# Joined column parts in three more jobs of the first MLP product, and one norm sum without spreading

## The chip, the cores and the metric

The kernel runs on one core of a Trainium2 chip. The metric is the device time of one execution in microseconds, the median of several. The engines are called as the profile calls them: PE (TensorE), DVE (VectorE), ACT (ScalarE), POOL (GpSimd), and SP, which here only issues DMAs.

## The reference

One encoder layer over 1536 tokens (a prompt sequence of 1024 and a sample sequence of 512), width 1024, all in float32:

```python
h = rms_norm(x, g_mix) * (1.0 + scale1) + shift1
z = h @ w_in                                  # 1024 x 1536
y_f = fourier_mixer(u_f, w_fourier)
y_r = bidirectional_rglru(conv(u_r), ...) * jax.nn.gelu(u_g)
mix = jnp.concatenate([y_f, y_r], axis=-1) @ w_out
x = x + gate1 * mix

h = rms_norm(x, g_mlp) * (1.0 + scale2) + shift2
ff = jnp.square(jax.nn.relu(h @ w_ff1)) @ w_ff2   # 1024 -> 4096 -> 1024
return x + gate2 * ff
```

and a last RMSNorm. shift, scale and gate come from a small product with the conditioning vector. The change lies in the second `rms_norm` and in `h @ w_ff1`.

## The kernel before

Activations lie transposed, 128 channels on the partitions and the tokens along the free dimension. The tokens are cut into three chunks of 512, taken in the order 0, 2, 1. Each engine has its own program, written out by hand in the order in which it runs; semaphores tie them together, and an engine that waits holds back everything behind it in its program.

**Products in two halves.** A float32 product is made of numbers split in a high part (`_hi`, rounded to fp32r) and a low part (`_lo`, the remainder): low weights by high data, high weights by low data, high by high (`three`, `three_of`, line 843 to 845). ACT makes the high part by a copy, DVE or POOL the low one by a subtraction (`split_w1_hi` on ACT, `w1_split_lo` on POOL, `token_lo` on DVE).

**The second norm.** While the output projection runs over its three chunks, ACT squares the new x, DVE adds the squares into `n_acc`, PE sums over the partitions (`norm_sum`), ACT takes the root (`root`), DVE the reciprocal (`rstd`), and DVE scales x (`norm_apply`). For the first chunk (n = NN) the sum is one product with the matrix of ones as weights and the 512 columns of `n_acc` as data, so that each partition has the sum of each column, and the reciprocal is one of 128x512. For the second and third chunk the sum is four products with 128 columns of `n_acc` as weights, the root and the reciprocal are of four columns, and PE spreads them to all partitions by four more products with the unit matrix (`norm_spread`, line 879).

**The first MLP product** uses a scheme of seven products for a 2x2 block product (Strassen and Winograd's): the tokens are halved into 768 columns each, the weights into blocks. There are 17 jobs: job 0 and job 5 are one pair of blocks in two halves, with 512 and with 256 columns; the other jobs have 768 columns, in two parts of 512 and 256 (a PSUM bank holds 512 columns of float32). In a job PE makes the seven products in the order P1, P5, P6, P2, P7, P3, P4 (i = 0 to 6), `ff1_product(q, i)`. P1, P6, P7 and P4 are added up in one PSUM buffer, and ACT copies the state of it after each (`ff1_out`, line 1636; semaphore `ff1_copy`). From these copies and the buffers of P5, P2 and P3 DVE makes the seven hidden blocks (`hid_out`, semaphore `hid_step`), in the steps U2, C11, B11, C22, B22, C12, B12, T1, T3, T2, T4; SP stores each to DRAM (`store_hid`, line 698). The weights of a product are in a ring of four places (`w1_hi`, `w1_lo`, `w1_s`); POOL makes the sums of weight blocks that P5, P6, P7 and P3 need (`w1_add`), but in job 5 DVE makes those of P7 and P3. SP loads the weights of the next job (`load_w1`, line 685), in its one queue between the stores.

**Joined parts.** In jobs 6 to 15 the part of 256 columns is done by `grouped` (line 854 and 857): four matmuls of 512 columns, high weights by high and low data side by side, and four of 256 columns, low weights by high data, which are added to the high columns. The result lies in two halves of 256 columns that DVE must add: `add_low(q, i)` (line 2294), and for P4 `relu_square(q)` on DVE, which in the other jobs is part of ACT's relu and square. The semaphore `ff1_added` counts these nine. In a joined job P6, P7 and P4 on PE wait for the addition of the product ahead of them in the same buffer, and P2 of the next job for that of P4; the store of the block `S_B21` waits for `relu_square`:

```python
if step: ...
else:
    sp.wait_ge(ff1_sq, q + 1)
    if QH <= q < NJ - 1:
        sp.wait_ge(ff1_added, added(q, SQ_P4))
```

For job 5 SP's order is: store of S_B21 of job 4, loads of job 6 (A11, A21, A22), store of S_T4 of job 4, load of A12.

Of the kernel before, what the change touches and what calls it, by code (L numbers as in the profile page):

```python
# [30 lines left out]
F32 = mybir.dt.float32  # L31
# [41 lines left out]
ADDED = (P1, P6, P5, P2, P7, A_P5, P3, P4, SQ_P4)  # L73
QH = REST + 2
U2, C11, B11, C22, B22, C12, B12, T1, T3, T2, T4 = range(1, 12)
# [73 lines left out]
def build_encoder(nc, vec_d, xT_d, w_mod_d, w_mod1_d, w_in_d, w_gate_d, w_four_d, w_out_d, w_ff1_d, w_ff2_d,  # L149
# [163 lines left out]
    n_acc = place("n_acc", [P, CH], F32, s2 + 2048)  # L313
    n_rstd = place("n_rstd", [P, CH], F32, A0 + HALF)
    n_sq = tmp[:2]
# [187 lines left out]
    def added(q, i):  # L503

        return len(ADDED) * (q - QH) + ADDED.index(i) + 1

# [31 lines left out]
    def spread_count(n):  # L538

        return n + 1 if n < NN else n  # L540

# [53 lines left out]
    def _(sp):  # L595
# [91 lines left out]
        def store_hid(q, j, step):  # L687

            pair, c0, c1 = JOBS[q]
            if step:  # L690
                sp.wait_ge(hid_step, NHID * q + step)
                if q == 0 and step in (B11, B22):
                    sp.wait_ge(first_relu, 2 if step == B11 else 6)
            else:
                sp.wait_ge(ff1_sq, q + 1)
                if QH <= q < NJ - 1:
                    sp.wait_ge(ff1_added, added(q, SQ_P4))
            sp.dma_start(hid_d[j, :, pair, c0:c1], hid_tile(j, q)[:, c0:c1]).then_inc(st_hid[j], 16)
# [135 lines left out]
    def _(pe):  # L834
# [26 lines left out]
        def norm_sum(n):  # L861

            pe.wait_ge(sq_added, adds_v(n + 1))
            if NN < n < 2 * NN:
                pe.wait_ge(xn_done, xn_count(n))
            if n == NN:
                pe.matmul(norm_bank(n)[:], ones[:], n_acc[:], start=True, stop=True).then_inc(norm_mm, 1)
                return
            total = squares(n)[:, 0, :] if shared(n) else n_acc[:]
            for b in range(4):  # L870
                m = pe.matmul(norm_bank(n)[:, b * P:(b + 1) * P], total[:, b * P:(b + 1) * P], ones[:],
                              start=True, stop=True)
            m.then_inc(norm_mm, 1)
# [238 lines left out]
        for i in range(1, NCH):  # L1112
            for d in range(KD):
                n = (i - 1) * KD + d

                pe.wait_ge(out_evac, n % 6 + 1 if n < 6 else KD + n - 5)
                if i == 2 and d == 0:
                    pe.wait_ge(mixr_lo, FT * 2)
                out_half(ORDER[i], d, 0, n % 6, True, False)
                if i == 2 and d == 0:  # L1120
                    norm_sum(NN + 1)
                out_half(ORDER[i], d, 1, n % 6, False, True).then_inc(out_mm, 1)
                if i == 1 and d == 0:
                    pe.wait_ge(out_evac, KD)
                    norm_sum(NN)
                elif i == 2 and d == 0:
                    norm_spread(NN + 1)

        def ff1_product(q, i):
# [10 lines left out]
            if i == P1:  # L1140
                after(pe, hid_step, NHID * (q - 1) + C11)
            elif i == P5:
                after(pe, hid_step, NHID * (q - 1) + C22)
            elif i == P2:
                after(pe, ff1_copy, 4 * q)
                if q > QH:
                    pe.wait_ge(ff1_added, added(q - 1, P4))
            elif i == P3:
                after(pe, hid_step, NHID * (q - 1) + C12)
            else:  # L1150
                pe.wait_ge(ff1_copy, 4 * q + {P6: 1, P7: 2, P4: 3}[i])
                if QH <= q < NJ - 1:
                    pe.wait_ge(ff1_added, added(q, {P6: P1, P7: P6, P4: P7}[i]))
# [4 lines left out]
            for part in parts:  # L1158
# [3 lines left out]
                begin = i in (P1, P5, P2, P3)  # L1162
                if part == 1 and QH <= q < NJ - 1:
                    m = grouped(ps[:, buf + CH:buf + 2 * CH],
                                [(w1_hi[o % 4][:, kk * P:(kk + 1) * P], w1_lo[o % 4][:, kk * P:(kk + 1) * P])
                                 for kk in range(FT)], lambda kk: pair[:, :, kk], begin, True)
                    continue
# [116 lines left out]
    def _(act):  # L1284
# [21 lines left out]
        def root(n):  # L1306
            act.wait_ge(norm_mm, n + 1)
            after(act, rc_done, n)
            if n == NN:
                act.activation(n_rstd[:], norm_bank(n)[:], ACT.Sqrt, bias=eps[:], scale=1.0 / D).then_inc(sd_done, 1)  # L1310
                return
            act.activation(sd[:], norm_bank(n)[:, 0:CH:P], ACT.Sqrt, bias=eps[:], scale=1.0 / D
                           ).then_inc(sd_done, 1)
# [308 lines left out]
        def ff1_out(q, i, j, step):  # L1622
# [4 lines left out]
            if q > 1 or i != P1:  # L1627
                after(act, hid_step, NHID * (q - 1) + step)
                after(act, st_hid[j], 16 * q)
            if i == P4 and QH <= q < NJ - 1:  # L1630
                act.activation(hid[j][:, CH:HTOK], ps[:, buf + CH:buf + HTOK], ACT.Copy)
# [200 lines left out]
        for d in range(2):  # L1832
            scale_small(d)
        act.wait_ge(norm_bc, 2 * NN + 2)
        act.activation(fin_s[:], bank[3][:, 0:QC], ACT.Copy).then_inc(small_r, 1)
# [6 lines left out]
    def _(dve):  # L1842
# [20 lines left out]
        def rstd(n):  # L1863

            dve.wait_ge(sd_done, n + 1)
            if n == NN:
                dve.reciprocal(n_rstd[:], n_rstd[:]).then_inc(rc_done, 1)
                return
# [336 lines left out]
        def norm_apply(n, tiles=range(KD)):  # L2205

            c = chunk_of(n)
            s = SEQ_OF[c]
            if n == NN:
                dve.wait_ge(rc_done, n + 1)  # L2210
            else:
                dve.wait_ge(norm_bc, spread_count(n))
            scale = n_rstd if n == NN else norm_bank(n)
            for k in tiles:
# [87 lines left out]
        def hid_out(q, step):  # L2302
# [8 lines left out]
            slot, at = [hid_tile(j, q) for j in range(7)], NHID * q  # L2311
            if QH <= q < NJ - 1 and step in (U2, C11, C22, C12, T4):
                dve.wait_ge(ff1_added, added(q, {U2: P5, C11: P2, C22: A_P5, C12: P3, T4: SQ_P4}[step]))
# [135 lines left out]
        def fin_rstd(h):  # L2449

            dve.wait_ge(sd_done, 2 * NN + h + 1)
            after(dve, norm_bc, (2 * NN - 1 + h) * h)
            dve.reciprocal(rc_half[:], sd_half[:]).then_inc(rstd_done, 1)
# [8 lines left out]
        def final_first(tiles):  # L2462

            dve.wait_ge(norm_bc, 2 * NN)
            final(tiles, 0, HTOK, ps[:, 6 * CH:6 * CH + HTOK])
# [6 lines left out]
        def final_small():  # L2472

            dve.wait_ge(norm_bc, 2 * NN + 1)
            r = bank[7][:, 0:QC].unsqueeze(1).to_broadcast([P, 2, QC])
# [31 lines left out]
        for q in range(1, NJ):  # L2507
            low = {U2: (P1, P6, P5), C11: (P2,), C22: (P7, A_P5), C12: (P3,)} if QH <= q < NJ - 1 else {}
            for step in (U2, C11, B11, C22, B22, C12, B12, T1, T3, T2):
# [4 lines left out]
                hid_out(q, step)  # L2514
            if QH <= q < NJ - 1:
                add_low(q, P4)
                relu_square(q)
            if q == REST:
                w1_add(q + 1, P7)
                w1_add(q + 1, P3)  # L2520
            hid_out(q, T4)

# [240 lines left out]
```

## Time and profile before

| | us |
|---|---|
| median of 3 runs (1399.94 to 1400.83) | 1400.32 |
| profiled execution | 1399.79 |
| its span, first to last instruction | 1397.5 |
| PE busy | 1376.4 (98%) |
| DVE busy | 848.4 (61%) |
| ACT busy | 586.6 (42%) |
| POOL busy | 477.7 (34%) |

The granted clock of PE is 0.999 over the span. The columns of a timeline are start in us from the span's start, duration in us, engine, line, operation, output<-input, shape and count; in brackets stands the idle time ahead of it and what ended it. Durations of matmuls overlap: it is the distance of their starts that counts.

### The profile page before, as it was taken

What the parts mean: (1) busy time and instruction counts of PE and PEld (TensorE: products, weight loads), DVE (VectorE), ACT (ScalarE), POOL (GpSimd) and SP (SyncE); (2) the same over time, 40 slices, a digit from 0 to 9 for tenths busy, and PEclk for the clock granted to TensorE, in tenths of its full rate; (3) what the DMA queues carried; (4) which work ended last, traced back from release to release, by engine and by line L of the source; (5) the groups of instructions that cost most, each with busy time, mean ns of one, the idle gap of its engine ahead of it and who ended that gap; (6) DMA issues with size and microseconds to landing.
All of it is one profiled execution on the core that took longest, in us unless ns stands there. A gap on an engine that the chain in (4) does not pass through costs nothing.

```text
span 1397.5 us, 17631 instructions
## 1 busy us (share of the span) xinstructions
PE 1376.4 (98%) x7050; PEld 1155.7 (83%) x7050; DVE 848.4 (61%) x871; ACT 586.6 (42%) x713; POOL 477.7 (34%) x269
## 2 busy tenths in 40 slices
PE   5999999999999999999999999999999999999998
PEld 4877778898888888888888888888888888888887
DVE  5967688795538974566545564453746434354584
ACT  5667888665325632232222222342322223423252
POOL 0002111145003775574554545531432222332131
PEclk9999999999999999999999999999999999999999
DMA  9444411106311343343433344479997444445552
GB/s 369 170 159 158 152 68 38 46 26 209 128 61 31 118 165 121 132 148 140 155 127 116 126 146 151 163 286 388 387 382 277 151 151 158 171 174 196 199 187 91
DMA packets 75698, 231.25 MB, mean 165 GB/s; under 512 B 5729, under 2 KB 9953, under 8 KB 66786
## 3 DMA queue, kind: packets, MB, share of 16 engines
q1 hardware_dynamic: 75074, 229.60, 44.9%
q8 instruction: 57, 0.93, 0.3%
q10 hardware_dynamic: 544, 0.52, 0.1%
q14 instruction: 23, 0.19, 0.0%
HBM read 165.09 MB, written 65.01 MB: 165 GB/s over the span
## 4 chain that ended last, share of the span: by engine, by line
PE 96%; DVE 2%; DMA 1%; issue 1%; SPq 1%; ACT 0%; POOL 0%; DVEq 0%; ACTq 0%
PE bank L844 17%; PE bank L843 17%; PE bank L845 17%; PE bank L854 10%; PE bank L837 9%; PE bank L838 9%; PE bank L839 9%; PE bank L857 5%; PE bank L889 1%; DMA win_raw<-in_w_in 1%; PE bank L901 0%; DVE two_r L2245 0%; SPq L604 0%; PE bank L910 0%; DVE n_t L2217 0%
## 5 line engine op out<-in xcount | busy, mean ns | idle before, releaser
L2387 DVE TENSOR_TENSOR hin_two<-hin,hin_two 128x3072 fp32r<-128x3072 f32 x28 | 131.4, 4694 | 185.7 <-ACT hin_two L1700 185.7
L2664 POOL TENSOR_TENSOR w_lo<-w_raw,w_hi 128x2048 fp32r<-128x2048 f32 x28 | 134.9, 4817 | 318.8 <-ACT w_hi L1688 317.2
L843 PE MATMUL bank<-hin_two,w_lo 128*128 128x512 f32 (+1 forms) x576 | 211.2, 367 | 0.0
L844 PE MATMUL bank<-hin_two,w_hi 128*128 128x512 f32 (+1 forms) x576 | 210.9, 366 | 0.0
L845 PE MATMUL bank<-hin_two,w_hi 128*128 128x512 f32 (+1 forms) x576 | 210.9, 366 | 0.0
L1688 ACT ACTIVATE w_hi<-w_raw 128x2048 fp32r<-128x2048 f32 x28 | 53.6, 1913 | 247.6 <-PE bank L857 149.5
L2656 POOL TENSOR_TENSOR w_lo<-w_raw,w_hi 128x512 fp32r<-128x512 f32 x43 | 63.3, 1473 | 180.1 <-ACT w_hi L1620 180.0
L845 PEld LDWEIGHTS bank<-hin_two,w_hi 128*128 128x128 f32 x576 | 108.6, 189 | 17.7
L843 PEld LDWEIGHTS bank<-hin_two,w_lo 128*128 128x128 f32 x576 | 108.7, 189 | 17.4 <-issue 0.2
L844 PEld LDWEIGHTS bank<-hin_two,w_hi 128*128 128x128 f32 x576 | 108.6, 189 | 17.4 <-issue 0.2
L2294 DVE TENSOR_TENSOR hid<-bank,hid 128x256 f32<-128x256 f32 x80 | 33.9, 424 | 124.2 <-ACT hid L1636 105.2
L2656 POOL TENSOR_TENSOR w_lo<-w_s,w_hi 128x512 fp32r<-128x512 f32 x68 | 105.0, 1561 | 7.2 <-ACT w_hi L1620 4.8
L2590 POOL TENSOR_TENSOR win_lo<-win_raw,win_hi 128x1024 fp32r<-128x1024 f32 x10 | 26.6, 2662 | 212.8 <-ACT win_hi L1325 212.8
L1636 ACT ACTIVATE hid<-bank 128x768 f32<-128x768 f32 (+2 forms) x58 | 44.4, 765 | 127.9 <-PE bank L845 82.0
L1700 ACT ACTIVATE hin_two<-hin 128x3072 fp32r<-128x3072 f32 x28 | 77.2, 2759 | 44.3 <-DMA hin<-hid_all 44.3
L844 PE MATMUL bank<-t_two,w_hi 128*128 128x512 f32 (+1 forms) x240 | 88.6, 369 | 0.0
L845 PE MATMUL bank<-t_two,w_hi 128*128 128x512 f32 (+1 forms) x240 | 88.6, 369 | 0.0
L843 PE MATMUL bank<-t_two,w_lo 128*128 128x512 f32 (+1 forms) x240 | 88.5, 369 | 0.0
L1620 ACT ACTIVATE w_hi<-w_s 128x512 fp32r<-128x512 f32 x68 | 43.0, 632 | 107.8 <-POOL w_s L2646 48.8
L854 PE MATMUL bank<-hin_two,w_hi 128*128 128x512 f32 x320 | 86.9, 393 | 0.0
L2332 DVE SCALAR_TENSOR_TENSOR hid<-hid 128x768 f32<-128x768 f32 (+1 forms) x48 | 66.1, 1377 | 1.7
L843 PE MATMUL bank<-two_f,w_lo 128*128 128x512 f32 (+1 forms) x176 | 63.6, 362 | 0.8 <-DVE hid L2321 0.4
(326 smaller groups left out, 3373.4 us busy)
## 6 DMA issues: line engine op xcount, KB each, us to landing
hin<-hid_all SPq DMA_DIRECT2D x28, 1536.0 KB, 6.7
hid_all<-hid SPq DMA_DIRECT2D x105, 384.0 KB, 2.4
w_raw<-in_w_ff SPq DMA_DIRECT2D x36, 1024.0 KB, 9.0
mod_raw<-in_w_mod SPq DMA_DIRECT2D x16, 1024.0 KB, 6.3
w_raw<-in_w_ff SPq DMA_DIRECT2D x60, 256.0 KB, 3.5
x<-in_xT SPq DMA_DIRECT2D x5, 2048.0 KB, 14.5
w_sums<-w_raw SPq DMA_DIRECT2D x8, 1024.0 KB, 15.5
w_raw<-w_sums SPq DMA_DIRECT2D x8, 1024.0 KB, 9.7
```

The source lines that it names most:

```text
L837: pe.matmul(out, w_lo, v_hi, start=first, stop=False)
L838: pe.matmul(out, w_hi, v_lo, start=False, stop=False)
L839: return pe.matmul(out, w_hi, v_hi, start=False, stop=last)
L843: pe.matmul(out, w_lo, v_hi, start=first, stop=False, skip_group_check=True)
L844: pe.matmul(out, w_hi, v_lo, start=False, stop=False, skip_group_check=True)
L845: return pe.matmul(out, w_hi, v_hi, start=False, stop=last, skip_group_check=True)
L854: pe.matmul(out.rearrange("p (h n) -> p h n", h=2), w_hi, v(t), start=first and t == 0, stop=False, skip_group_check=True)
L857: m = pe.matmul(out[:, HI * QC:(HI + 1) * QC], w_lo, v(t)[:, HI], start=False, stop=last and t == len(weights) - 1, skip_group_check=True)
L1700: act.activation(hin_part(n % 3, HI), hin[n % 3][:].rearrange("p t n -> p (t n)"), ACT.Copy).then_inc(hin_hi_done, 1)
L2387: dve.tensor_tensor(hin_part(n % 3, LO), hin[n % 3][:].rearrange("p t n -> p (t n)"), hin_part(n % 3, HI), ALU.subtract).then_inc(hin_lo_d ...
L2656: pool.tensor_tensor(w1_lo[o % 4][:], src[:], w1_hi[o % 4][:], ALU.subtract).then_inc(w1_lo_done, 1)
L2664: pool.tensor_tensor(w2_lo[n % 2][:].rearrange("p t n -> p (t n)"), w2_raw[m % RAWS][:].rearrange("p t n -> p (t n)"), w2_hi[n % 2][:].rea ...
```

## The change

Two changes. The list of joined jobs, before all from 6 to 15, becomes `JOINED`, jobs 2, 3, 4 and 6 to 15; every place that asked for `QH <= q < NJ - 1` asks for `q in JOINED`. In job 4 DVE's two weight sums for job 5 now stand ahead of its addition of P4 and its relu-square. And the second chunk of the second norm (n = NN + 1) is summed like the first, by one product with ones, with a root and a reciprocal of 128x512 and no `norm_spread`; the counts on `norm_bc` fall by one.

```diff
-QH = REST + 2
+JOINED = tuple(q for q in range(2, NJ - 1) if q != REST + 1)
...
-    n_rstd = place("n_rstd", [P, CH], F32, A0 + HALF)
+    n_rstd = [place(f"n_rstd{i}", [P, CH], F32, o) for i, o in enumerate((A0 + HALF, A0 + 2 * HALF + 11 * 2048))]
...
-        return len(ADDED) * (q - QH) + ADDED.index(i) + 1
+        return len(ADDED) * JOINED.index(q) + ADDED.index(i) + 1
...
-        return n + 1 if n < NN else n
+        return min(n + 1, NN) if n < NN + 2 else n - 1
...
-                if QH <= q < NJ - 1:
+                if q in JOINED:
                     sp.wait_ge(ff1_added, added(q, SQ_P4))
...
-            if n == NN:
+            if n in (NN, NN + 1):
                 pe.matmul(norm_bank(n)[:], ones[:], n_acc[:], start=True, stop=True).then_inc(norm_mm, 1)
                 return
...
                 if i == 1 and d == 0:
                     pe.wait_ge(out_evac, KD)
                     norm_sum(NN)
-                elif i == 2 and d == 0:
-                    norm_spread(NN + 1)
...
             elif i == P2:
                 after(pe, ff1_copy, 4 * q)
-                if q > QH:
+                if q - 1 in JOINED:
                     pe.wait_ge(ff1_added, added(q - 1, P4))
...
-                if QH <= q < NJ - 1:
+                if q in JOINED:
                     pe.wait_ge(ff1_added, added(q, {P6: P1, P7: P6, P4: P7}[i]))
...
-                if part == 1 and QH <= q < NJ - 1:
+                if part == 1 and q in JOINED:
                     m = grouped(ps[:, buf + CH:buf + 2 * CH],
...
-            if n == NN:
-                act.activation(n_rstd[:], norm_bank(n)[:], ACT.Sqrt, bias=eps[:], scale=1.0 / D).then_inc(sd_done, 1)
+            if n in (NN, NN + 1):
+                act.activation(n_rstd[n - NN][:], norm_bank(n)[:], ACT.Sqrt, bias=eps[:], scale=1.0 / D).then_inc(sd_done, 1)
...
-            if i == P4 and QH <= q < NJ - 1:
+            if i == P4 and q in JOINED:
                 act.activation(hid[j][:, CH:HTOK], ps[:, buf + CH:buf + HTOK], ACT.Copy)
...
-            if n == NN:
-                dve.reciprocal(n_rstd[:], n_rstd[:]).then_inc(rc_done, 1)
+            if n in (NN, NN + 1):
+                dve.reciprocal(n_rstd[n - NN][:], n_rstd[n - NN][:]).then_inc(rc_done, 1)
...
-            scale = n_rstd if n == NN else norm_bank(n)
+            scale = n_rstd[n - NN] if n < NN + 2 else norm_bank(n)
...
-            low = {U2: (P1, P6, P5), C11: (P2,), C22: (P7, A_P5), C12: (P3,)} if QH <= q < NJ - 1 else {}
+            low = {U2: (P1, P6, P5), C11: (P2,), C22: (P7, A_P5), C12: (P3,)} if q in JOINED else {}
...
-            if QH <= q < NJ - 1:
-                add_low(q, P4)
-                relu_square(q)
             if q == REST:
                 w1_add(q + 1, P7)
                 w1_add(q + 1, P3)
+            if q in JOINED:
+                add_low(q, P4)
+                relu_square(q)
             hid_out(q, T4)
```

## Rows read from the trace of the kernel before

**Rows 1.** Page, busy us, share of the span, instructions of each engine.

```profile
PE 1376.4 (98%) x7050; PEld 1155.7 (83%) x7050; DVE 848.4 (61%) x871; ACT 586.6 (42%) x713; POOL 477.7 (34%) x269
```

**Rows 2.** PE's waits, whole run: who for whom, us in total, times, longest us.

```profile
PE bank L843 <- DVE hid L2321: 0.4, 1, 0.4
...
PE bank L843 <- POOL w_lo L2656: 0.4, 1, 0.4
```

**Rows 3.** PE's timeline, job 2: start us, us, what; parts apart.

```profile
524.04 0.28 PE L843 MATMUL bank<-two_f,w_lo 128*128 128x256 f32 x1
...
532.38 0.28 PE L843 MATMUL bank<-t4b_two,w_lo 128*128 128x256 f32 x1
...
532.50 0.28 PE L844 MATMUL bank<-t4b_two,w_hi 128*128 128x256 f32 x1
```

**Rows 4.** PE's timeline, job 6: starts of two joined groups.

```profile
613.99 0.39 PE L854 MATMUL bank<-t_two,w_hi 128*128 128x512 f32 x1
...
622.26 0.62 PE L854 MATMUL bank<-two_f,w_hi 128*128 128x512 f32 x2
```

**Rows 5.** PE's timeline at the norm's sums and its spreading.

```profile
369.50 1.02 PE L867 MATMUL bank<-n_acc,ones 128*128 128x512 f32 x2
...
370.59 0.40 PE L838 MATMUL bank<-lo_r,wo_hi 128*128 128x512 f32 x1
...
411.21 1.05 PE L871 MATMUL bank<-ones,n_acc 128*128 128x128 f32 x8
...
414.83 1.05 PE L879 MATMUL bank<-ident,rc 128*128 128x128 f32 x8
...
415.95 0.39 PE L838 MATMUL bank<-lo_r,wo_hi 128*128 128x512 f32 x1
```

**Rows 6.** DVE's timeline: first reciprocal, x of the third chunk, idle in brackets.

```profile
371.28 3.35 DVE L1867 RECIPROCAL n_rstd<-n_rstd 128x512 f32<-128x512 f32 x1 [0.76 <-ACT n_rstd L1310]
...
415.03 0.75 DVE L2257 SCALAR_TENSOR_TENSOR x<-bank,mod,x 128x512 f32<-128x512 f32 x1 [2.20 <-PE bank L839]
...
454.04 0.75 DVE L2257 SCALAR_TENSOR_TENSOR x<-bank,mod,x 128x512 f32<-128x512 f32 x1 [1.89 <-PE bank L839]
```

**Rows 7.** Timelines of DVE and PE where job 2 begins.

```profile
512.61 0.96 DVE L2354 TENSOR_TENSOR hid<-hid,hid 128x768 f32<-128x768 f32 x1
...
512.98 0.39 PE L843 MATMUL bank<-t_two,w_lo 128*128 128x512 f32 x1
```

**Rows 8.** Page: group of the additions of 256 columns.

```profile
L2294 DVE TENSOR_TENSOR hid<-bank,hid 128x256 f32<-128x256 f32 x80 | 33.9, 424 | 124.2 <-ACT hid L1636 105.2
```

**Rows 9.** PE's timeline: starts of (6,P1) and (6,P5).

```profile
602.88 0.40 PE L843 MATMUL bank<-two_f,w_lo 128*128 128x512 f32 x1
...
607.02 1.19 PE L854 MATMUL bank<-t_two,w_hi 128*128 128x512 f32 x4
```

**Rows 10.** DVE's timeline, from job 4 to job 5.

```profile
595.71 0.69 DVE L2366 TENSOR_TENSOR w_s<-w_raw,w_s 128x512 f32<-128x512 f32 x1
...
596.31 0.95 DVE L2354 TENSOR_TENSOR hid<-hid,hid 128x768 f32<-128x768 f32 x1
...
598.68 1.26 DVE L2332 SCALAR_TENSOR_TENSOR hid<-hid 128x256 f32<-128x256 f32 x1
```

**Rows 11.** POOL's timeline: low halves of (5,P7) and (6,P1).

```profile
596.42 1.99 POOL L2656 TENSOR_TENSOR w_lo<-w_s,w_hi 128x512 fp32r<-128x512 f32 x1 [1.36 <-ACT w_hi L1620]
...
601.18 1.48 POOL L2656 TENSOR_TENSOR w_lo<-w_raw,w_hi 128x512 fp32r<-128x512 f32 x1
```

**Rows 12.** SP: loads of job 6; landing of its first, and of job 5's three.

```profile
595.64 0.82 SPq L685 DMA_DIRECT2D w_raw<-in_w_ff  x2
...
DMA to landing us min/median/max: 4.4/4.4/4.4
...
DMA to landing us min/median/max: 2.6/3.3/3.6
```

**Rows 13.** ACT's timeline: high half for (6,P1).

```profile
600.48 0.62 ACT L1620 ACTIVATE w_hi<-w_raw 128x512 fp32r<-128x512 f32 x1
```

More of the change, by code:

```diff
@@ L1833, in _ @@
             scale_small(d)
-        act.wait_ge(norm_bc, 2 * NN + 2)
+        act.wait_ge(norm_bc, 2 * NN + 1)
         act.activation(fin_s[:], bank[3][:, 0:QC], ACT.Copy).then_inc(small_r, 1)
@@ L2208, in norm_apply @@
             s = SEQ_OF[c]
-            if n == NN:
+            if n in (NN, NN + 1):
                 dve.wait_ge(rc_done, n + 1)
@@ L2311, in hid_out @@
             slot, at = [hid_tile(j, q) for j in range(7)], NHID * q
-            if QH <= q < NJ - 1 and step in (U2, C11, C22, C12, T4):
+            if q in JOINED and step in (U2, C11, C22, C12, T4):
                 dve.wait_ge(ff1_added, added(q, {U2: P5, C11: P2, C22: A_P5, C12: P3, T4: SQ_P4}[step]))
@@ L2451, in fin_rstd @@
             dve.wait_ge(sd_done, 2 * NN + h + 1)
-            after(dve, norm_bc, (2 * NN - 1 + h) * h)
+            after(dve, norm_bc, (2 * NN - 2 + h) * h)
             dve.reciprocal(rc_half[:], sd_half[:]).then_inc(rstd_done, 1)
@@ L2462, in final_first @@
         def final_first(tiles):
-            dve.wait_ge(norm_bc, 2 * NN)
+            dve.wait_ge(norm_bc, 2 * NN - 1)
             final(tiles, 0, HTOK, ps[:, 6 * CH:6 * CH + HTOK])
@@ L2472, in final_small @@
         def final_small():
-            dve.wait_ge(norm_bc, 2 * NN + 1)
+            dve.wait_ge(norm_bc, 2 * NN)
             r = bank[7][:, 0:QC].unsqueeze(1).to_broadcast([P, 2, QC])
```

## The prediction

> **What bounds the kernel now.** I read the page's busy shares first: TensorE (PE) is busy 98% of the 1397.5 us span, DVE 61% [rows 1]. So nothing that DVE, ACT or POOL do counts by its length, only where PE has to wait for it. Then I read PE's waits over the whole run. In the part that the change touches there are just two, of 0.4 us each: the first product of the second job waits for DVE (474 us), and a product of the sixth job waits for POOL's low half of its weights (598.5) [rows 2]. Then PE's timeline, product by product, in a job with separate parts [rows 3] and in one with joined parts [rows 4]; then DVE, POOL and SP around the places where the change puts a new wait. So each edit is priced twice: what PE issues less, and whether PE now reaches a semaphore before its giver does.
>
> I call the jobs by their number q (third to fifth are q = 2, 3, 4; q = 5 is the short one of 256 columns; q = 6 to 15 are joined already), and a product by job and name, (2,P6). Times on the clock are those of the trace of before.
>
> **Part 1, joined products on PE.** In each of the 7 products of jobs 2, 3 and 4, twelve matmuls of 256 columns become four of 512 and four of 256: the same 3072 columns, in 8 instructions and not 12. As neighbouring products run their parts in opposite order, two products make a period. Separate: from 524.04 to 532.38, 8.34 us, in which one of 256 columns takes 0.12 (532.38 to 532.50) and so one of 512 takes (8.34 - 24 x 0.12) / 24 = 0.228 [rows 3]. Joined: from 613.99 to 622.26, 8.27 us [rows 4]. So a product gains 0.035 us and 21 of them 0.7 us. I take off 0.05, because a first joined group stands between products of the other kind: **-0.65 us**. Bounds: the joining brings nothing (0), or four matmuls fewer by the price that they have over their columns, 2 x 0.120 - 0.228 = 0.012 us each, 0.05 a product: -1.05.
>
> A rule speaks against this part. The Trainium skill, "TensorE: Matmul & The Clock Gate", section "Back-to-back issue gap", gives an isolated matmul N/2.4 + 2.5 ns. By it four instructions less would save only 10 ns a product, an estimate of 0.2 us for 21, and the change would come out 0.45 us later than my sum. The rows of this kernel, 8.34 against 8.27, say 35 ns, and I go by them.
>
> **Part 2, the norm.** The spreading of the second chunk stands on PE at 414.83; to the second matmul behind it, at 415.95, pass 1.12 us, of which the first takes 0.23, so it costs 0.89. The sum at 411.21 is four products of the same shape, and I give it the same 0.89. The first chunk is already done by one product with ones as weights: 369.50 to 370.59, 1.09 - 0.23 = 0.86 [rows 5]. The change makes the sum 0.86 for 0.89 and drops the spreading: **-0.92 us**. PE's waits [rows 2] hold neither, so it is all length.
> The price is on DVE: a reciprocal of 512 columns, 3.35 us as in the first chunk, for one of 4 columns. There it began 1.78 us after the product (371.28 against 369.50, the root on ACT between them); so here it runs from 413.0 to 416.4, and what stood at 415.03 (the new x of the third chunk, then eight scalings) starts 1.4 us later [rows 6]. Those who read it are the ACT shifts and the token sums, and PE wants none of them before the first MLP product, 40 us on. DVE stands idle 1.89 us before 454.04, waiting for PE [rows 6], so it has caught up there even with PE 0.92 us ahead. I cost it at nothing; if that cover were gone, the whole 1.2 to 1.4 us would reach the second job's first product, where PE waits for DVE already. From 454 to 475 DVE works without a gap, started by PE, so that old wait moves ahead with PE and stays 0.4 us long.
>
> **Part 3, the new wait in job 2.** In a joined job DVE has to add the halves of P1 before PE may write P6 into the same buffer (the wait on ff1_added, value P1). DVE reaches job 2 late: it still has the token sums of job 1 to make, works without a gap up to the last step of job 1, T4 at 512.61, 0.96 us, and ends it at 513.57. The addition takes 0.42 us [rows 8], with the hand-over 513.6 to 514.1. PE begins (2,P6) at 512.98 [rows 7], and would by the gain of part 1 be there 0.07 us earlier. So PE waits 514.1 - 512.9: **+1.15 us**. Both sides move ahead by the same 0.92 of part 2, so it doesn't matter here. Bounds: 0.7 (DVE's chain is 0.4 us shorter because locks fall otherwise) and 1.6. Jobs 3 and 4 are cut like 7 and 8 of before, in which PE waits for nothing [rows 2], and I give them no cost.
> The edit also puts nine DVE operations into each job (eight of 0.42 us and one relu-square): 3.8 us of DVE time in seven products of 4.2. DVE has the room; only the order matters.
>
> **Part 4, jobs 4 to 6.** Job 5 has a third of a job's columns and lasts some 10 us, so what DVE, POOL and SP prepare for it and for job 6 has no slack. Three things come in. (a) PE's (5,P2) now waits for the addition of (4,P4), which DVE makes after the two weight sums: the second at 595.71, 0.69 long, so the addition ends at 596.8. Counted back from (6,P1) at 602.88 [rows 9], three products of 12 x 0.12 = 1.44 us put (5,P7) at 598.5; ahead of it are the old wait for POOL, some 0.5, and (5,P2) itself, which so began at 596.5. It now waits 0.3 us, and the old wait behind it falls. (b) relu-square of job 4 then follows on DVE, with both inputs in SBUF. At 596.42 POOL begins the low half of (5,P7); DVE's T4 of 0.95 us at 596.31 was ahead of it [rows 10] and made it last 1.99 us [rows 11]. Without T4 there I take 1.3, 0.7 less. Now POOL comes first and DVE waits: relu-square ends at 597.7 + 0.4 = 598.1. That is what the trace does to such pairs: the 256-column relu-square at 598.68 took 1.26 us beside POOL [rows 10], where an addition of that size out of PSUM takes 0.42 [rows 8]. The Trainium skill says so, "SBUF — State Buffer", section "SBUF: two separate sides": an exclusive lock for the whole instruction, which a DVE operation with two SBUF inputs and one of POOL take from each other. By that rule, the trace agrees.
> (c) SP stores job 4's square (hid, B21) first, and the weight loads of job 6 stand behind it in its queue. The store now waits for relu-square, 598.1, not for ACT's square. The load of A11 was issued at 595.64 and landed 4.4 us later, at 600.04 [rows 12]; now the store is issued first, 0.4 us as two loads took 0.82, and the load at 598.5, and lands after some 3.3 us, as the median of three such loads did at 568.7 [rows 12], at 601.8. ACT's split took 0.62 us and started at 600.48 [rows 13]; now it ends at 602.4. POOL's low half, 1.48 us [rows 11], ends at 603.9. PE began (6,P1) at 602.88 [rows 9]: now 603.9. From there POOL makes two sums and the low half of P5 without a gap, from 601.18 + 1.48 = 602.66 [rows 11] to the start of (6,P5) at 607.02 [rows 9], 4.36 us: now 603.9 + 4.36 = 608.3. **+1.25 us** at (6,P5), which takes in (a), the freed 0.5 us and what job 4's last product had gained. Bounds: the load lands in 2.6 us and POOL is at once free: +0.5; relu-square slips in ahead of POOL and the chain is POOL's own, as before: 0; the load takes 4.4 us again and T4 of job 4, 0.95 us, takes POOL's lock in the middle of the chain: +3.2.
> PE's waits show nothing behind job 5 in this product [rows 2], so nothing is carried on but the shift.
>
> **The sum.** -0.65 - 0.92 + 1.15 + 1.25 = +0.83 us. The profiled execution of before took 1399.79 us (span 1397.5 and 2.3 around it): 1400.6. The median of the three runs shown is 0.53 above that execution, so for the median **1401.1 us**. A slower or faster reading than 0.2%, 2.8 us, is about what a measurement can tell from no change.
>
> **Rivals.**
> A, the wait for the weights of job 6 is hidden: loads land early or relu-square comes before POOL's lock. Then part 4 is about +0.1, and the sum -0.3: 1400.0. For it: at 598 the stores of job 4 are mostly through. Against: the chain through ACT and POOL has no spare time.
> B, neither new wait shows: DVE ends job 1 earlier than PE reaches (2,P6), and job 5 runs without its old wait. -0.65 - 0.92 - 0.5 = -2.1: 1398.3. For it: the norm's cover. Against: what DVE has left in job 1 is its own work, which nothing in the change makes shorter.
> C, the other side, slower: at job 6 the SP queue and the lock add up, with the load at 4.4 us and T4 in POOL's chain, +3.2 for +1.25. The point of decision is whether POOL has (6,P1)'s low half by 604.5. Sum +2.8: 1403.1.
> D, the joining gains nothing in jobs 2 to 4: each group's four instructions less are lost again in the block of 512 columns behind it. Then the 0.65 falls away: 1401.8. For it: 35 ns a product are a small difference of two long periods. Against: the period is the same in every pair of job 6. The rule of part 1 comes near to this case.
> E, the change doesn't do what it says for the norm: the reciprocal of 3.35 us delays DVE up to the second job and PE gives the 0.92 back there: 1402.0.
>
> **Chances and range.** Forecast 0.55, own range 1400.2 to 1401.9; A 0.17; B 0.06; C 0.13; D 0.05; E 0.04. The range takes in A, D, E and all of C but its far end, and the runs' own spread of 0.4 us: 1399.3 to 1403.1. Faster by over 2.8 us has 0.02 (B and more), slower by over 2.8 has 0.11 (the upper half of C and what I don't see), within 0.87.
>
> **What the profile after would show.** Groups of four and four in 21 products ahead of 592, with a period of 8.27; no spreading near 414 and a DVE reciprocal of 3.35 us there; a PE wait of about 1.1 us for DVE's low addition near 513; a small one for it near 596; the old wait for POOL near 598.5 gone; a PE wait near 603 of about 1 us for POOL, behind an SP load issued some 2.8 us later than before. What would make me wrong: DVE done with T4 of job 1 before PE reaches (2,P6); the load issued before 597; or a PE wait in jobs 3, 4 or in the second job longer than 0.4.

## The result, and the profile after

| | before | changed |
|---|---|---|
| median of 22 runs, us | 1400.01 | 1401.83 |
| lowest and highest, us | 1399.59 to 1400.83 | 1400.90 to 1405.49 |
| ratio to before, 95% interval | | 1.0017 (1.0010 to 1.0023) |
| profiled execution, us | 1399.79 | 1404.35 |

The change makes the kernel 1.8 us slower, and the times now spread over 4.6 us, where before's 22 lie within 1.2. The profiled execution is one of the long ones, 2.5 us above the median. Its waits are the same in kind as those of e10, a second profile of the changed kernel at 1401.47 us, but longer. I call a run of 1401 to 1402 us an ordinary one.

The page, span and busy times (as [rows 1]):

```profile
span 1402.4 us, 17486 instructions
...
PE 1376.4 (98%) x6952; PEld 1150.9 (82%) x6952; DVE 854.8 (61%) x898; ACT 587.0 (42%) x716; POOL 478.6 (34%) x269
```

PE is busy for the same 1376.4 us as before, to a tenth, although two pieces of work are gone from it: 1.7 us are added by a stretch of slower matmuls behind job 5 (below). What makes the span 4.9 us longer is nearly all in PE's waits, of the whole run (as [rows 2]: who for whom, us in total, times, longest):

```profile
PE bank L843 <- POOL w_lo L2654: 3.6, 1, 3.6
...
PE bank L843 <- issue: 1.3, 2, 1.0
...
PE bank L843 <- DVE hid L2319: 0.4, 1, 0.4
```

A wait of 3.6 us for POOL stands where one of 0.4 was; 1.0 us called "issue" is new as well; the wait for DVE at the second job is the same 0.4.

**The norm.** PE's and DVE's timelines at the second chunk (as [rows 5] and [rows 6]):

```profile
411.19 1.02 PE L867 MATMUL bank<-n_acc,ones 128*128 128x512 f32 x2
...
413.04 3.35 DVE L1865 RECIPROCAL n_rstd<-n_rstd 128x512 f32<-128x512 f32 x1 [2.16 <-ACT n_rstd L1308]
...
416.31 0.65 DVE L2255 SCALAR_TENSOR_TENSOR x<-bank,mod,x 128x512 f32<-128x512 f32 x1
```

One product stands where there were two groups of eight matmul records, and no spreading follows it. The reciprocal runs from 413.04 to 416.39, and the new x of the third chunk, at 415.03 before, starts at 416.31. DVE still stands idle for 1.89 us before the last chunk's first x, now at 453.09, and the second job's first product waits for DVE for 0.4 us as before, so the delay has been made good by then.

**Joined jobs.** PE's timeline in job 2, the starts of two joined groups (as [rows 4]):

```profile
516.00 0.39 PE L854 MATMUL bank<-t_two,w_hi 128*128 128x512 f32 x1
...
524.27 0.62 PE L854 MATMUL bank<-two_f,w_hi 128*128 128x512 f32 x2
```

The period is 8.27 us, as in job 6 of before, against 8.34.

**Job 2.** DVE's low addition of (2,P1) and PE's timeline there (as [rows 7]):

```profile
512.53 0.41 DVE L2292 TENSOR_TENSOR hid<-bank,hid 128x256 f32<-128x256 f32 x1
...
511.77 0.39 PE L845 MATMUL bank<-t_two,w_hi 128*128 128x512 f32 x1
...
513.16 0.47 PE L843 MATMUL bank<-t_two,w_lo 128*128 128x512 f32 x1 [1.00 <-issue]
...
513.47 0.39 PE L844 MATMUL bank<-t_two,w_hi 128*128 128x512 f32 x1
```

DVE's addition ends at 512.94, and PE starts (2,P6) at 513.16. From 511.77 to 513.47 two matmuls take 1.70 us where they need 0.46: PE lost 1.24 us, 1.16 of it before (2,P6) starts and 0.08 in its first matmul, which takes 0.31 and not 0.23. The profile calls the wait "issue" and names no giver, but the addition is what this product waits for in the program, and it ends 0.2 us ahead; in e3 and e5, where job 2 isn't joined, the wait is gone.

**Jobs 4 to 6.** DVE's addition and relu-square of job 4, SP's first loads of job 6 and the landing of the first, then ACT's high half, POOL's low half and PE's (6,P1) (as [rows 9 to 13]):

```profile
595.97 0.42 DVE L2292 TENSOR_TENSOR hid<-bank,hid 128x256 f32<-128x256 f32 x1
...
596.42 1.22 DVE L2298 SCALAR_TENSOR_TENSOR hid<-hid 128x256 f32<-128x256 f32 x1
...
598.13 1.75 SPq L685 DMA_DIRECT2D w_raw<-in_w_ff  x2
...
DMA to landing us min/median/max: 6.0/6.0/6.0
...
604.21 0.63 ACT L1618 ACTIVATE w_hi<-w_raw 128x512 fp32r<-128x512 f32 x1 [4.08 <-DMA w_raw<-in_w_ff]
...
604.91 1.26 POOL L2654 TENSOR_TENSOR w_lo<-w_raw,w_hi 128x512 fp32r<-128x512 f32 x1 [4.14 <-ACT w_hi L1618]
...
606.23 0.63 PE L843 MATMUL bank<-two_f,w_lo 128*128 128x512 f32 x1 [3.64 <-POOL w_lo L2654]
...
612.05 1.09 PE L854 MATMUL bank<-t_two,w_hi 128*128 128x512 f32 x4
```

The chain that the prediction names, link by link: relu-square takes 1.22 us beside POOL and ends at 597.64; SP issues the store, then the load at 598.13, 2.5 us later than before; it lands after 6.0 us, where before it took 4.4; ACT begins when it has landed (its bracket names the DMA), POOL after ACT, PE after POOL. PE stood for 3.64 us. And then it runs slower. Four stretches of 2 us follow (busy time and count of PE, PEld, DVE, ACT, POOL, then the granted clock, DMA share, GB/s):

```profile
604.00:606.00 2.00, 0.00 (x0) 0.00 (x0) 0.00 (x0) 0.63 (x1) 1.09 (x1) 1.00 1.04 391
...
606.00:608.00 2.00, 1.77 (x5) 1.39 (x6) 0.00 (x0) 0.50 (x1) 1.87 (x3) 0.61 0.52 181
...
608.00:610.00 2.00, 2.00 (x7) 1.59 (x6) 0.00 (x0) 1.19 (x4) 1.86 (x2) 0.53 0.01 4
...
610.00:612.00 2.00, 2.00 (x12) 1.72 (x11) 1.43 (x1) 0.78 (x2) 2.00 (x3) 1.00 0.19 66
```

The granted clock falls to 0.61 and 0.53 of full speed, that is to the lower of its two levels, 1.2 GHz, for most of 4 us, and is back at 2.4 GHz from 610. The first matmuls stand 0.43 us apart there and not 0.23. From the start of (6,P1) to that of (6,P5) pass 5.82 us (606.23 to 612.05), where before it was 4.14 (602.88 to 607.02): 1.7 us more.

### The profile page after: what moved, and what is told of

It reads as the page before. It is cut to its first block, busy times and chain, and to the rows that moved or that the text cites. A ratio compares the mean times of both kernels' runs of the same rounds, so it can differ in the third digit from the quotient of the medians.

```text
span 1402.4 us, 17486 instructions
## 1 busy us (share of the span) xinstructions
PE 1376.4 (98%) x6952; PEld 1150.9 (82%) x6952; DVE 854.8 (61%) x898; ACT 587.0 (42%) x716; POOL 478.6 (34%) x269
## 4 chain that ended last, share of the span: by engine, by line
PE 56%; POOL 0%; issue 0%; DVE 0%; ACT 0%; DVEq 0%; POOLq 0%; ACTq 0%
PE bank L844 14%; PE bank L845 14%; PE bank L843 14%; PE bank L854 10%; PE bank L857 5%; POOL w_lo L2654 0%; DVE x L2477 0%; PE bank L1270 0%; PE bank L1192 0%; PE bank L1185 0%; PE bank L1252 0%; PE bank L1276 0%; ACT w_hi L1618 0%; DVEq L2701 0%; PE bank L1262 0%
## 5 line engine op out<-in xcount | busy, mean ns | idle before, releaser
L2292 DVE TENSOR_TENSOR hid<-bank,hid 128x256 f32<-128x256 f32 x104 | 44.1, 424 | 160.6 <-ACT hid L1634 135.8
L845 PEld LDWEIGHTS bank<-hin_two,w_hi 128*128 128x128 f32 x576 | 108.6, 189 | 17.7
L844 PEld LDWEIGHTS bank<-hin_two,w_hi 128*128 128x128 f32 x576 | 108.7, 189 | 17.4 <-issue 0.2
L843 PE MATMUL bank<-t_two,w_lo 128*128 128x512 f32 (+1 forms) x216 | 81.8, 379 | 1.0 <-issue 1.0
L845 PE MATMUL bank<-t_two,w_hi 128*128 128x512 f32 (+1 forms) x216 | 81.9, 379 | 0.0
L844 PE MATMUL bank<-t_two,w_hi 128*128 128x512 f32 (+1 forms) x216 | 81.9, 379 | 0.0
L854 PEld LDWEIGHTS bank<-hin_two,w_hi 128*128 128x128 f32 x320 | 56.1, 189 | 8.6
L843 PE MATMUL bank<-two_f,w_lo 128*128 128x512 f32 (+1 forms) x152 | 57.5, 378 | 4.1 <-POOL w_lo L2654 3.6
```

The source lines that it names most:

```text
L843: pe.matmul(out, w_lo, v_hi, start=first, stop=False, skip_group_check=True)
L844: pe.matmul(out, w_hi, v_lo, start=False, stop=False, skip_group_check=True)
L845: return pe.matmul(out, w_hi, v_hi, start=False, stop=last, skip_group_check=True)
L854: pe.matmul(out.rearrange("p (h n) -> p h n", h=2), w_hi, v(t), start=first and t == 0, stop=False, skip_group_check=True)
L2292: dve.tensor_tensor(part, ps[:, 2 * CH * buf + HTOK:2 * CH * (buf + 1)], part, ALU.add).then_inc(ff1_added, 1)
```

## The experiments

Before was run beside each; its medians were 1399.93 or 1399.94 us, of 15 or 33 runs.

### The norm alone (e1)

```diff
-JOINED = tuple(q for q in range(2, NJ - 1) if q != REST + 1)
+JOINED = tuple(range(REST + 2, NJ - 1))
```

> Joined jobs as before (6 to 15), only the norm's part of the change. Theory (each part has its own price, the norm's is 0.92 us less on PE, DVE's longer reciprocal is covered): 1399.1 us, 0.9 under before, with DVE's reciprocal from 413.0 to 416.4 and PE's first product of the second job 0.9 us earlier than before. Rival (the reciprocal's delay reaches the second job): within 0.2 us of before, 1400.0, with a PE wait for DVE near 475 longer than 0.4 us.

Measured 1399.15 us (11 runs, 1398.83 to 1399.58), ratio 0.9994 (0.9986 to 1.0003). That is 0.8 under before; the interval just reaches no change, but PE's wait at the second job was 0.4 us, which rules the rival out. The norm is no part of the loss, and most likely a gain of its own.

### The store behind the loads (e2)

```diff
             if q > 0:
-                store_hid(q - 1, S_B21, 0)
+                if q != REST + 1:
+                    store_hid(q - 1, S_B21, 0)
...
                 load_w1(q + 1, (A11, A21, A22) if q else (A11, A21))
+                if q == REST + 1:
+                    store_hid(q - 1, S_B21, 0)
```

> The change, but SP issues job 4's B21 store behind the three weight loads of job 6, not ahead of them. Theory (the loads stood behind a store that waits for DVE's relu-square): the loads are issued near 595.3 again, PE waits for POOL's low half of (6,P1) by less than 0.6 us, and the time falls from 1401.8 to 1399.6 to 1400.0. Rival (POOL's lock against DVE in job 5 makes the low half late, whenever the loads come): PE still waits 1 us or more, 1401.0 or more.

Measured 1399.06 us (1398.70 to 1399.53), ratio 0.9994 (0.9985 to 1.0003). SP's first loads of job 6, and the landing of the first two:

```profile
595.37 0.81 SPq L685 DMA_DIRECT2D w_raw<-in_w_ff  x2
...
DMA to landing us min/median/max: 2.8/3.2/3.6
```

The loads are issued at 595.37, land after 2.8 and 3.6 us, and PE no longer waits for POOL near 603. One statement moved in SP's program takes 2.8 us off the change, more than the whole of its loss, and the times lie within 0.8 us again. That is 0.5 us below the 1399.6 that I had named as the low end; why is taken up with the sum below. The rival, POOL's lock alone, would have kept the wait; it falls.

### Job 2 left out (e3)

```diff
-JOINED = tuple(q for q in range(2, NJ - 1) if q != REST + 1)
+JOINED = tuple(q for q in range(3, NJ - 1) if q != REST + 1)
```

> The change with jobs 3 and 4 joined, job 2 not. Theory (job 2's wait for DVE's low addition costs 1.28 us, the joining of a job gives 0.25): 1.0 us under the change, 1400.8, and no PE wait near 512. Rival (DVE is just as late one job later): a PE wait for the low addition of (3,P1) of about the same length, and the change's own 1401.8.

Measured 1401.47 us (1400.57 to 1403.01): 0.36 under the change, not 1.0. PE's waits from 400 to 700 us, and the landing of the first load:

```profile
PE bank L843 <- POOL w_lo L2654: 2.1, 1, 2.1
...
PE bank L843 <- issue: 0.3, 1, 0.3
...
DMA to landing us min/median/max: 4.5/4.5/4.5
```

The wait of job 2 is gone (what is left of "issue" is the 0.3 in job 5), so it was not handed on to job 3, and the rival falls; but the wait for POOL at (6,P1) is 2.1 us here, behind a landing of 4.5 us, where e10 has 1.7 and 0.2. The 11 runs also fall into two groups (see e8), so that their median says little about 1 us; the expected 1400.8 is missed all the same. The same step without it is e5.

### Job 4 left out (e4)

```diff
-JOINED = tuple(q for q in range(2, NJ - 1) if q != REST + 1)
+JOINED = tuple(q for q in range(2, NJ - 1) if q not in (REST, REST + 1))
```

> The change with jobs 2 and 3 joined, job 4 not. Theory (all that the change loses around job 6 comes from job 4's relu-square on DVE and what waits for it): from (4,P4) on PE runs as before, with the 0.4 us wait for POOL in job 5 back: 1400.0 - 0.92 - 0.45 + 1.28 = 1399.9. Rival (the loss around job 6 comes of PE being earlier or DVE busier at large): 1401 or more, PE wait of over 1 us at (6,P1).

Measured 1399.76 us (1399.32 to 1400.69), ratio 1.0 (0.9991 to 1.0009), as the theory's sum has it. The waits of PE are job 2's 1.0, and 0.4 each for DVE and for POOL as in before. So the loss around job 6 comes from job 4 being joined, and not from PE being earlier.

### Both repairs (e5)

e2, with the list of e3.

> Norm part, jobs 3 and 4 joined and not job 2, and the B21 store of job 4 behind the weight loads of job 6. Theory (job 2's wait is 1.3 us of PE time that nothing gives back, the joining of job 2 brings 0.25): 1.0 us under e2_store_behind, 1398.0 us, no PE wait near 512 and none above 0.6 near 603; it is then the fastest of all. Rival (PE, earlier by 1 us in job 3, meets another wait on DVE or POOL): 1399.0, with that wait in the trace.

Measured 1398.17 us (1398.06 to 1398.95), ratio 0.9988 (0.9980 to 0.9997): the fastest of all, 1.8 us under before, and 0.89 under e2 for the 1.0 expected. PE's waits from 400 to 700 us:

```profile
PE bank L846 <- DVE hid L2322: 0.4, 1, 0.4
...
PE bank L846 <- issue: 0.3, 1, 0.3
```

That is all that PE waits there: 0.4 for DVE at the second job, and 0.3 for the addition of (4,P4) in job 5. Here job 2's wait is worth what its trace says.

### The late store alone, in the kernel before (e6)

The edit is to the kernel before.

```diff
                 if QH <= q < NJ - 1:
                     sp.wait_ge(ff1_added, added(q, SQ_P4))
+                if q == REST:
+                    sp.wait_ge(hid_step, NHID * q + T4)
```

> The kernel before, with one wait more on SP and nothing else: the B21 store of job 4 waits for DVE's T4 of job 4 (ends 597.3), so that the loads of job 6 behind it are issued near 597.8 and not at 595.64. Theory (the loads' place in SP's queue alone makes the loss): slower than before by 0.5 to 2.5 us, 1400.5 to 1402.5, PE wait for POOL at (6,P1) near 603, and a wider spread of times than before's 0.8. Rival (the loss needs the joined job's work on DVE): 1400.0, no such wait.

Measured 1402.01 us (1401.16 to 1403.74), ratio 1.0018 (1.0010 to 1.0027). SP's loads, the first landing, PE's waits for POOL, the first and seventh matmul of (6,P1), and two stretches of 2 us, of an execution of 1403.72 us:

```profile
597.86 0.89 SPq L685 DMA_DIRECT2D w_raw<-in_w_ff  x2
...
DMA to landing us min/median/max: 4.9/4.9/4.9
...
PE bank L845 <- POOL w_lo L2658: 2.3, 2, 1.9
...
605.06 0.50 PE L845 MATMUL bank<-two_f,w_lo 128*128 128x512 f32 x1 [1.92 <-POOL w_lo L2658]
...
606.57 0.58 PE L845 MATMUL bank<-two_f,w_lo 128*128 128x512 f32 x1
...
606.00:608.00 2.00, 2.00 (x8) 1.59 (x7) 0.00 (x0) 0.87 (x2) 1.73 (x3) 0.65 0.54 180
...
608.00:610.00 2.00, 2.00 (x7) 1.54 (x6) 0.80 (x1) 1.60 (x4) 2.00 (x2) 0.50 0.02 8
```

One wait on SP, with none of jobs 2 to 4 joined and no work added to any engine, costs 2.1 us and brings the wide spread with it, and the clock at its lower level too. It falls only 1.5 us after PE has resumed: six matmuls stand about 0.23 us apart, and from the seventh on it is 0.4. This is the cost of the late store by itself, and it is larger than the 1.25 that I had put on it.

### DVE's old order (e7)

```diff
-            if q == REST:
-                w1_add(q + 1, P7)
-                w1_add(q + 1, P3)
             if q in JOINED:
                 add_low(q, P4)
                 relu_square(q)
+            if q == REST:
+                w1_add(q + 1, P7)
+                w1_add(q + 1, P3)
```

> The change with DVE's order of job 4 as it was: addition of P4 and relu-square ahead of the two weight sums for job 5. The B21 store is then released near 595 and the loads of job 6 are issued 2.5 us earlier than in the change; but the weight sums come 0.9 to 1.5 us later. Theory: PE waits for POOL in job 5 at (5,P7) 1.5 to 2 us instead of 0.5, and the waits at (6,P1) shrink to under 1 us: 1400.5 to 1401.5, with a narrow spread. Rival (the order of the sums matters more than the loads): 1402 or more.

Measured 1399.64 us (1399.34 to 1399.92), ratio 0.9997 (0.9988 to 1.0006), 2.2 us under the change and 0.9 under the low end of my theory. DVE's addition, relu-square and first weight sum, SP's loads, and PE's wait for POOL from 590 to 612 us:

```profile
593.76 0.42 DVE L2292 TENSOR_TENSOR hid<-bank,hid 128x256 f32<-128x256 f32 x1
...
594.22 1.07 DVE L2298 SCALAR_TENSOR_TENSOR hid<-hid 128x256 f32<-128x256 f32 x1
...
595.21 0.68 DVE L2361 TENSOR_TENSOR w_s<-w_raw,w_raw 128x512 f32<-128x512 f32 x1
...
595.91 0.83 SPq L685 DMA_DIRECT2D w_raw<-in_w_ff  x2
...
PE bank L843 <- POOL w_lo L2654: 0.8, 1, 0.8
```

The relu-square ends at 595.29 and frees the store; the loads go at 595.91. The weight sum behind it, which I feared for, ends at 595.89, only 0.6 us later than in the change (595.26), and 0.3 of that is the whole trace being later: ahead of relu-square it took 1.78 us beside POOL's low half, and behind it, with that low half done at 595.00, it takes 0.68. PE's wait for POOL is the old one in job 5, at (5,P7): 0.8 us, half of what I expected, and at (6,P1) it waits for nothing. With job 4 joined, then, the place of the two sums ahead of relu-square decides whether the store is late.

### Work for PE in its wait (e8)

```diff
+            if q == REST + 2 and i == P1:
+                pe.wait_ge(hid_step, NHID * (q - 1) + C11)
+                for _ in range(10):
+                    pe.matmul(ps[:, buf:buf + P], ident[:], ones[:], start=True, stop=True)
             pe.wait_ge(w1_lo_done, o + 1)
```

> The change, with ten small products of constants put on PE ahead of its wait for (6,P1)'s weights (about 2.0 us of PE work, whose results are overwritten). Theory (the wait for POOL is 1 to 4 us by the landing of the load, and where it is long PE's granted clock falls afterwards and adds up to 1.7 us): the slow end of the times, 1402.6 to 1405.5 in the change, comes down to under 1404, the fast end rises by 0.5 to 1, and the profile shows no clock under 1 near 606. Rival (the spread is the landing alone): all times rise by 0 to 1 us, the slow end too.

Measured 1401.92 us (11 runs, 1401.28 to 1403.32). Two stretches of 2 us behind the wait:

```profile
604.00:606.00 2.00, 2.00 (x14) 1.71 (x14) 1.13 (x1) 0.00 (x0) 1.80 (x2) 1.00 1.03 397
...
606.00:608.00 2.00, 2.00 (x11) 1.65 (x10) 0.00 (x0) 0.78 (x2) 1.72 (x3) 1.00 0.72 252
```

The clock stays at 1.00. Of the change's 22 runs 9 lie at 1402.6 or above, here one of 11; the highest is 2.2 us lower and the lowest 0.4 higher, a little less than the 0.5 to 1 that the theory has. The profile fell on a run of 1401.54, so it doesn't show a long wait with the clock kept.

The granted clock is on record for each run, as a mean over its span. The three kernels with the late store and no filler fall into two groups by time:

| | lower group: runs, median us, clock | upper group: runs, median us, clock |
|---|---|---|
| change | 13, 1401.44, all 0.999 or 1.000 | 9, 1403.77, eight 0.997 or 0.998, one 0.999 |
| e3 | 6, 1400.93, all 0.999 or 1.000 | 5, 1402.65, all 0.997 or 0.998 |
| e6 | 6, 1401.62, all 0.999 or 1.000 | 5, 1403.56, four 0.997 or 0.998, one 0.999 |

No run of the lower groups has a mean under 0.999, and 17 of the 19 in the upper ones do. The groups are 1.7 to 2.3 us apart, about the 1.7 us that (6,P1) loses at the lower clock. With the filler ten of 11 runs have 0.999 or 1.000; the eleventh, the one of 1403.32, has 0.949, which no trace explains. So the wide spread is mostly the clock. That the clock falls because PE waits is borne out by the filler; why it falls in one execution and not in the next isn't shown.

### Late loads, with the store behind them (e9)

e2, and ahead of the loads of job 6:

```diff
+                if q == REST + 1:
+                    sp.wait_ge(ff1_added, added(q - 1, SQ_P4))
```

> The change, with the B21 store of job 4 behind the loads of job 6 as in e2_store_behind, but the loads themselves held back by a wait for relu-square. So they are issued as late as in the change (near 597.8), and only the store of 384 KB is no longer ahead of them. Theory one (the late issue is the loss, and the landing of 4.5 to 6 us is that stretch's own): 1401.0 to 1401.8, PE wait near 603 of over 1 us, landing over 4 us. Theory two (the store ahead of the loads makes their landing 6 instead of 3.3 us, as I had reckoned): landing near 3.3, PE wait under 0.7, 1399.6 to 1400.3.

Measured 1400.27 us (1399.81 to 1400.76), ratio 1.0004 (0.9994 to 1.0013). SP's loads, the first landing, PE's wait for POOL:

```profile
597.84 1.98 SPq L685 DMA_DIRECT2D w_raw<-in_w_ff  x2
...
DMA to landing us min/median/max: 3.2/3.2/3.2
...
PE bank L848 <- POOL w_lo L2659: 0.5, 1, 0.5
```

Theory two holds, at the upper end of its range. The loads are nearly as late as in the change (597.84 against 598.13 and, in e10, 598.37), but the first lands after 3.2 us, and PE waits 0.5. So the loss has two halves: the late issue, 1400.27 - 1399.06 = 1.2 us, and the store of 384 KB ahead of the loads in the same queue, 1401.83 - 1400.27 = 1.6 us. The second takes in that the loads go 0.3 to 0.5 us earlier without the store's issue ahead of them, and about 0.4 of it are the runs at the lower clock (against the lower group of the change, 1401.44, it is 1.2). The split is for a late issue: issued early, the load may stand behind the store at little cost, as in e7, where it lands after 4.7 us and (6,P1) doesn't wait.

### The change again (e10, e11)

> The changed kernel once more, for a second profile of it. If the spread of its times comes from the landing of the load of A11 and the clock after PE's wait, a run of 1401 to 1402 shows the load landing at about 5 us or less, a PE wait near 603 under 2.5 us and a granted clock of 1.00 behind it; a run above 1403 shows 6 us and more, a wait above 3 us and the clock near half. If the two have nothing to do with it, a run of 1401 to 1402 may show the long wait too.

> As e10_change_again, for a third profile: the same relation of landing, wait and clock to the run's time.

They took 1401.47 and 1401.68 us, ordinary runs both, with the same waits. Of e10: SP's first loads, landing of the three, ACT's high half, POOL's first sum for (6,P5), PE's (4,P4) from its part of 256 columns, (6,P1) and (6,P5), and a stretch of 2 us:

```profile
598.37 1.70 SPq L685 DMA_DIRECT2D w_raw<-in_w_ff  x2
...
DMA to landing us min/median/max: 3.8/4.3/4.5
...
602.30 0.63 ACT L1618 ACTIVATE w_hi<-w_raw 128x512 fp32r<-128x512 f32 x1 [1.93 <-DMA w_raw<-in_w_ff]
...
604.78 1.44 POOL L2630 TENSOR_TENSOR w_s<-w_raw,w_raw_even 128x512 f32<-128x512 f32 x1 [0.33 <-DMA w_raw_even<-in_w_ff]
...
590.64 1.07 PE L854 MATMUL bank<-t4b_two,w_hi 128*128 128x512 f32 x4
...
604.51 0.50 PE L843 MATMUL bank<-two_f,w_lo 128*128 128x512 f32 x1 [1.68 <-POOL w_lo L2654]
...
609.13 1.19 PE L854 MATMUL bank<-t_two,w_hi 128*128 128x512 f32 x4 [0.20 <-POOL w_lo L2654]
...
606.00:608.00 2.00, 2.00 (x10) 1.64 (x9) 0.00 (x0) 0.89 (x2) 1.73 (x3) 1.00 0.67 234
```

The first load lands after 3.8 us (e11: 3.8), PE waits 1.7 us at (6,P1) and 0.2 more at (6,P5), and the clock stays at 1.00. The long run of the profile above has 6.0 us, 3.6 us and the lower clock. In these three profiles a run of 1401 to 1402 goes with the short landing and one of 1404 with the long one, as expected. But e6's profile, a run of 1403.72, has a landing of 4.9 and a wait of 1.9 us only, with the lower clock: of the two, the clock is what the long runs have in common.

## Why the prediction was right, point by point

The forecast was slower by 0.8 us, 1401.1, with a range of 1399.3 to 1403.1. Measured: slower by 1.8, 1401.83. So direction, places and causes were right, and the forecast size was less than half of what came.

**The joined products**, -0.65. Right: the period in job 2 is 8.27 us. Rival D, no gain at all, falls by that, though its time, 1401.8, is the one measured. The rule of the Trainium skill for an isolated matmul ("TensorE: Matmul & The Clock Gate", section "Back-to-back issue gap"), from which I had estimated 10 ns a product, is not borne out by the 35 ns of the trace.

**The norm**, -0.92. Right within what can be measured: e1 gives 0.8. Rival E (DVE's delay reaches the second job) falls by the unchanged 0.4 us wait.

**Job 2**, +1.15. Right in place, cause and size: 1.24 in the trace, 0.89 net in e5 against e2, where 1.24 - 0.25 = 1.0 is to be expected. The wait up to the start of (2,P6) is the 1.15 forecast, within 0.01; the 0.1 beyond is the first matmul behind it, which takes 0.31 us and not 0.23.

**Jobs 4 to 6**, +1.25. The mechanism was right and the term mis-sized. I count from the start of the 256-column part of (4,P4) to that of (6,P5). In before that part starts at

```profile
590.76 0.28 PE L843 MATMUL bank<-t4b_two,w_lo 128*128 128x256 f32 x1
```

The ordinary run e10 loses 2.2 us against before (609.13 - 590.64 against 607.02 - 590.76), 1.0 more than forecast, and the profiled one 5.4. By its steps: relu-square's end was right (598.1 forecast, 597.9 in e10), and so was the issue of the load (598.5 and 598.37). The step that was mis-sized is the landing. It was put at 3.3 us, by a row of loads with no store right ahead of them. Behind the store it is 3.8 in the ordinary run, 4.9 in e6 and 6.0 in the profiled one; and the third load, which POOL's first sum needs, lands at 604.6, so POOL waits 0.33 us more for it. I had used the quiet row as the value and 4.4 as the far end, and the far end was still too near. These are 0.8 of the 1.0 us; hand-overs of about 0.1 us between DMA, ACT, POOL and PE make up the rest. The clock was left out altogether: I had priced only the wait, not what PE does after it.

**The sum** with the sizes of the ordinary run: -0.65 - 0.92 + 1.24 + 2.2 = +1.9. The span of e10 is 2.1 us longer than that of before (1399.6 against 1397.5), which fits. That the medians differ by 1.8 as well is partly chance, as two things that the sum leaves out cancel. The runs at the lower clock lift the change's median from 1401.44 to 1401.83. And the time outside the span, which I had held at 2.3 us, is 1.9 in e10 and 2.0 in e2, 0.3 to 0.4 less, which no run here explains. It is also most of why e2 came out below what I expected, since its span, 1397.1, is 0.4 under before's and its time 0.7.

There was luck in the range too. I had added to the median of three runs, 1400.32, where that of 22 is 1400.01. My own range, 1400.2 to 1401.9, holds the measured time by 0.07 us; worked out from 1400.01 it would have ended at 1401.6, short of it.

Rival A (the wait for the weights is hidden) is refuted by e6 and e10, B by job 2's wait. Rival C had the right mechanism at a size of 3.2, but T4 in POOL's chain was no part of it: with the weights missing POOL was idle, and T4 cost nothing. The runs above 1403.1, of which the change has 7 in 22, lie at its time, but in large part by the clock (e8), which it doesn't name.

What I hadn't weighed is the order on DVE. With the weight sums first, the old wait for POOL in job 5 goes, as forecast; with them second (e7) it grows to 0.8 us, but the store is free about 2.5 us earlier and the whole is 2.2 us faster.

## What to carry to other kernels

When a block gets an additional step on one engine, look at what its store stands in front of in the DMA queue: here a relu-square moved from ACT to DVE, which had time to spare (61% busy), cost 2 to 3 us (2.1 in e6, 2.8 between the change and e2), because the next job's weight loads waited behind its store, and moving one line of SP's program gave all of it back. Early loads make up for a slow landing, late ones don't. Price a load by its landing behind the traffic that the change puts in front of it, not by the median of quiet ones. And a saving of 0.035 us a product pays for a joined job only where the adding engine is not behind: job 2 gained 0.25 us and lost 1.24.

## What the runs showed of the hardware

The first load of job 6, of 256 KB, landed after 2.8 us (e2), 2.9 (e5) and 3.2 (e9, issued late) where no store was issued right ahead of it. Behind the store of 384 KB it took 4.4 (before), 4.5 (e1), 4.7 (e7) and 5.1 (e4) when issued between 595.1 and 596, and 3.8 (e10 and e11), 4.4 (e8), 4.5 (e3), 4.9 (e6) and 6.0 (profiled execution) when issued between 597.3 and 598.7. Why the same program has 3.8 in one execution and 6.0 in another stays open. After PE's idle of 3.6 us the granted clock was at its lower level for most of 4 us, and 1.7 us were added to the wait. In e6 it was so after a wait of 1.9 us, also at a price of 1.7 us (605.06 to 610.91 from (6,P1) to (6,P5), where before has 4.14), and in e10 and e3 it was not, after 1.7 and 2.1; what decides between them stays open. And the same weight sum of DVE, 128x512 with both inputs in SBUF, took 1.78 us where it started beside POOL's low half (the change) and 0.68 where it started after it (e7), so that moving it behind the relu-square cost it almost nothing.
